# State-space stage of a hybrid encoder block on eight cores: two sets of LT broadcast tiles, and the CW/KF preparation split into two parts

## The reference, cut to what matters

```
def _s5_direction(u, lam_re, lam_im, log_dt, b_re, b_im, c_re, c_im, reverse):
    ...
    dt = jnp.exp(log_dt.astype(f32))[:, None]
    lam_bar = jnp.exp(lam * dt)
    ...
    b_bar = ((lam_bar - 1.0) / lam)[..., None] * b_mat
    ...
    bu = jnp.einsum('gph,blgh->blgp', b_bar, u.astype(jnp.complex64))
    a = jnp.broadcast_to(lam_bar, bu.shape)
    _, states = lax.associative_scan(_linear_recurrence_op, (a, bu), reverse=reverse, axis=1)
    return jnp.einsum('ghp,blgp->blgh', c_mat, states).real
```

## Time and profile before

| | us |
|---|---|
| median of 12 runs | 1573.94 |
| lowest and highest of them | 1569.84, 1695.45 |
| the profiled execution | 1569.84 |
| its span on the slowest core, from first to last instruction | 1568.7 |
| spans of the eight cores | 1561.8 to 1568.7 |

### The profile page before, as it was taken

How to read it: one execution, slowest core, us unless ns; L and a number is a source line. 1 busy time by engine, 2 the same in 40 slices (tenths; PEclk the granted TensorE clock), 3 DMA queues, 4 the chain that set the end, 5 groups by cost and what they waited for, 6 DMA issues and landing times.

```text
span 1568.7 us, 21398 instructions; the slowest of 8 cores (1561.8 to 1568.7 us)
## 1 busy us (share of the span) xinstructions
PE 1115.2 (71%) x6296; PEld 596.9 (38%) x6296; DVE 759.5 (48%) x1262; ACT 594.8 (38%) x1111; POOL 546.3 (35%) x582
## 2 busy tenths in 40 slices
PE   1988747995517731763256346488899999999995
PEld 1434313442405521552245234244344444444442
DVE  2374521113484738563756466456234443334456
ACT  2778633223314451536252625456211111111134
POOL 1000001222194638473657379300332333333231
PEclk9999979998555565565556556699899999999998
DMA  9523300000100000000000000082421430332114
GB/s 194 118 68 102 91 2 0 1 1 0 34 2 20 1 1 21 1 1 1 14 1 0 1 1 1 14 199 71 68 34 22 54 55 4 51 55 28 27 55 161
DMA packets 27377, 61.77 MB, mean 39 GB/s; under 512 B 2272, under 2 KB 11104, under 8 KB 27264
## 3 DMA queue, kind: packets, MB, share of 16 engines
q0 software_dynamic: 15408, 22.58, 10.5%
q1 hardware_dynamic: 11856, 37.82, 7.6%
HBM read 74.58 MB, written 8.39 MB: 53 GB/s over the span
## 4 chain that ended last, share of the span: by engine, by line
PE 57%; DVE 13%; ACT 13%; issue 10%; POOL 4%; DMA 2%; ACTq 0%; DVEq 0%; POOLq 0%; SPq 0%
PE p_pb L936 14%; PE p_pb L954 14%; PE p_pb L461 6%; PE p_pb L680 5%; PE p_pb L579 4%; DVE s_smb L272 4%; PE p_pb L876 4%; PE p_pb L413 2%; DMA s_w_in_bf<-w_in 2%; ACT s_CD L448 2%; PE p_pb L397 1%; PE p_pb L401 1%; DVE s_tbt L700 1%; DVE s_CD L451 1%; PE p_pb L842 1%
## 5 line engine op out<-in xcount | busy, mean ns | idle before, releaser
L958 DVE TENSOR_TENSOR s_h<-s_h,p_pb 128x512 f32<-128x512 f32 x256 | 175.7, 688 | 259.1 <-PE p_pb L954 258.2
L940 POOL TENSOR_TENSOR s_hid<-s_rl 128x512 bf16<-128x512 f32 x128 | 133.3, 1044 | 337.2 <-ACT s_rl L939 308.3
L936 PE MATMUL p_pb<-s_zffn,s_w1c 128*128 128x512 bf16 x1024 | 228.4, 382 | 3.4 <-issue 3.4
L954 PE MATMUL p_pb<-s_w2c,s_hid 128*128 128x512 bf16 x1024 | 227.8, 381 | 4.3 <-DVE s_h L958 4.3
L939 ACT ACTIVATE s_rl<-p_pb 128x512 f32<-128x512 f32 x128 | 76.2, 597 | 341.1 <-PE p_pb L936 321.7
L680 PE MATMUL p_pb<-s_u_s,s_WB 32*128 32x257 bf16 (+1 forms) x768 | 160.1, 406 | 49.4 <-ACT s_VAbig L685 46.9
L936 PEld LDWEIGHTS p_pb<-s_zffn,s_w1c 128*128 128x128 bf16 x1024 | 100.7, 98 | 126.0 <-issue 6.9
L954 PEld LDWEIGHTS p_pb<-s_w2c,s_hid 128*128 128x128 bf16 x1024 | 100.5, 98 | 126.5 <-issue 6.9
L680 PEld LDWEIGHTS p_pb<-s_u_s,s_WB 32*128 32x128 bf16 x768 | 102.2, 139 | 103.0 <-issue 57.2
L461 PE MATMUL p_pb<-s_uc,s_CD 128*128 128x512 bf16 x496 | 114.8, 394 | 32.2 <-DVE s_CD L451 32.2
L579 PE MATMUL p_pb<-s_identf,s_LTt 128*128 128x128 f32 x256 | 65.5, 437 | 86.7 <-ACT s_LTt L576 61.5
(11 more groups left out here) (153 smaller groups left out, 1793.6 us busy)
## 6 DMA issues: line engine op xcount, KB each, us to landing
s_xt<-xl SPq DMA_DIRECT2D x32, 512.0 KB, 3.8
s_h<-xl SPq DMA_DIRECT2D x16, 512.0 KB, 19.9
s_w1c<-w_ff POOLq DMA_DIRECT2D x8, 1024.0 KB, 14.1
s_w2c<-w_ff POOLq DMA_DIRECT2D x8, 1024.0 KB, 14.4
out<-s_h SPq DMA_DIRECT2D x16, 512.0 KB, 2.7
s_w_in_bf<-w_in POOLq DMA_DIRECT2D x8, 384.0 KB, 20.0
s_w_out_bf<-w_out POOLq DMA_DIRECT2D x1, 2048.0 KB, 47.3
s_bc<-b_c SPq DMA_DIRECT2D x4, 256.0 KB, 4.1
```

The lines of the kernel that those rows point to most:

```text
L936: op("pe", lambda e, k=k, f=f: e.matmul(pb[pi_][:, :], w1c[wb_][:, k, f * 128:(f + 1) * 128], zffn[:, k, blk * 512:(blk + 1) * 512], start ...
L940: op("pool", lambda e, f=f: e.tensor_tensor(hid[hb][:, f, :], rl[rb][:], rl[rb][:], op=ALU.mult), r=["rl%d" % rb], w=["hid%d_%d" % (hb, f)])
L954: op("pe", lambda e, f=f, half=half: e.matmul(pb[pi_][:, :], hid[hb][:, f, ti * 128:(ti + 1) * 128], w2c[wb_][:, f, half * 512:(half + 1) ...
L958: op("dve", lambda e, half=half: e.tensor_tensor(h[:, tt_, half * 512:(half + 1) * 512], h[:, tt_, half * 512:(half + 1) * 512], pb[pi_][: ...
```

## The change

`LTt` gets eight buffers in two sets, chosen by whether the power is even or odd, and ACT's copies for the next power are written ahead of PE's matmuls of the present one, within one half. `bc` keeps a single buffer. `prep_cwkf` gets a parameter: part "a" holds the loads, the CW products, Bb and C0 and stays behind tile 1; part "b" holds the KF matmuls, the KF copies and Dd and is written behind tile 6, which puts it behind V7 on PE and behind table 7 on ACT. The cut diff (Bb and C0 are only indented):

```diff
@@ -523,12 +523,12 @@
-            bcs = [P.sb("bc%d" % i, [128, 2, 2, 128], F32) for i in range(2)]
+            bcs = [P.sb("bc0", [128, 2, 2, 128], F32)] * 2
...
-            LTt = [P.sb("LTt%d" % i, [128, 4, 32], F32) for i in range(4)]
+            LTt = [P.sb("LTt%d" % i, [128, 4, 32], F32) for i in range(8)]
...
-                bc = bcs[jj % 2]
-                bck = "bc%d" % (jj % 2)
+                bc = bcs[0]
+                bck = "bc0"
                 if half in (None, 0):
                     P.dma("sp", bc[:], b_c_d[:, jj], w=[bck])
-                for e_ in range(8):
-                    if half is not None and e_ // 4 != half:
-                        continue
+                es = [e_ for e_ in range(8) if half is None or e_ // 4 == half]
+
+                def lt_copies(e_):
+                    for ri in range(2):
+                        for dl in range(2):
+                            li = (e_ % 2) * 4 + ri * 2 + dl
+                            qv = Qk[e_][ri]
+                            o0 = jj * 8 + dl * 4
+                            op("act", lambda e, li=li, qv=qv, o0=o0: e.copy(
+                                LTt[li][:], qv.ap[:, o0:o0 + 4].unsqueeze(2).to_broadcast([128, 4, 32])), r=[qv.key], w=["LT%d" % li])
+
+                lt_copies(es[0])
+                for e_ in es:
+                    if e_ + 1 in es:
+                        lt_copies(e_ + 1)
                     pw = e_ % 4
                     for ri in range(2):
                         for dl in range(2):
-                            lt = LTt[ri * 2 + dl]
-                            ltk = "LT%d" % (ri * 2 + dl)
-                            qv = Qk[e_][ri]
-                            o0 = jj * 8 + dl * 4
-                            op("act", lambda e, lt=lt, qv=qv, o0=o0: e.copy(
-                                lt[:], qv.ap[:, o0:o0 + 4].unsqueeze(2).to_broadcast([128, 4, 32])), r=[qv.key], w=[ltk])
+                            li = (e_ % 2) * 4 + ri * 2 + dl
+                            lt = LTt[li]
+                            ltk = "LT%d" % li
                             col = (ri * 2 + dl) * 128
                             op("pe", lambda e, lt=lt, col=col, pw=pw: e.matmul(
                                 pb[pw][:, col:col + 128], lt[:].rearrange("p a b -> p (a b)"), identf[:], start=True, stop=True),
...
-            def prep_cwkf(jj):
-                P.dma("sp", cs[:], c_s_d[:, jj], w=["cs"])
-                P.dma("sp", bs[:], b_s_d[:, jj], w=["bs"])
+            def prep_cwkf(jj, part=None):
+                if part in (None, "a"):
+                    P.dma("sp", cs[:], c_s_d[:, jj], w=["cs"])
+                    P.dma("sp", bs[:], b_s_d[:, jj], w=["bs"])
...
                 for k in range(1, 9):
+                    if part == "b":
+                        break
                     pre_, pim_ = Pk[k]
                     ce = "pool" if k % 2 == 0 else "dve"
                     Ba, Bc = (B3, B4) if k % 2 == 0 else (B1, B2)
...
+                if part == "b":
+                    pass
+                else:
+                  qre, qim = Qk[0]
+                  tt("dve", B1, bsre, bc8(qre), ALU.mult)
...
+                if part == "a":
+                    return
                 for k in range(8):
                     for dl in range(2):
                         for q in range(4):
...
@@ -764,7 +781,9 @@
                     if i < 8:
                         emit_scan(i)
                     if i == 1:
-                        prep_cwkf(jj)
+                        prep_cwkf(jj, "a")
+                    if i == 6:
+                        prep_cwkf(jj, "b")
                     if i == 3 and jj < 3:
                         prep_wb(jj + 1, 0)
                     if i == 5 and jj < 3:
```

More of the change, by code:

```diff
@@ L614, in prep_cwkf @@
                                                                        op=ALU.subtract), r=[Ba.key, Bc.key], w=[cwk])
[L615 to L626, removed]
+                if part == "b":
[3 more added lines that the diff above has]
+                  tt("dve", B1, bsre, bc8(qre), ALU.mult)
+                  tt("dve", B2, bsim, bc8(qim), ALU.mult)
+                  op("dve", lambda e: e.tensor_tensor(Bb[:, 0].rearrange("p a b c -> p (a b) c"), B1.ap, B2.ap, op=ALU.subtract),
+                     r=[B1.key, B2.key], w=["Bb"])
+                  tt("dve", B1, bsre, bc8(qim), ALU.mult)
+                  tt("dve", B2, bsim, bc8(qre), ALU.mult)
+                  op("dve", lambda e: e.tensor_tensor(Bb[:, 1].rearrange("p a b c -> p (a b) c"), B1.ap, B2.ap, op=ALU.add),
+                     r=[B1.key, B2.key], w=["Bb"])
+                  op("dve", lambda e: e.tensor_copy(C0[:, 0].rearrange("p a b c -> p (a b) c"), csre.ap), r=["cs"], w=["C0"])
+                  op("dve", lambda e: e.tensor_scalar(C0[:, 1].rearrange("p a b c -> p (a b) c"), csim.ap, -1.0, None, op0=ALU.mult),
+                     r=["cs"], w=["C0"])
+                if part == "a":
+                    return
                 for k in range(8):
```

## The result

| | us |
|---|---|
| median before (32 runs beside these) | 1573.94 |
| median after (8 runs) | 1524.35 |
| ratio, with its 95% interval | 0.9694 [0.9684, 0.9704] |
| profiled execution before, after | 1569.84, 1522.89 |
| its span before, after | 1568.7, 1521.8 |

The account below looks back on a forecast made before the run. In the state-space stage, all engines queue behind DVE's part a, and LT copies wait for PE. Gains 3.9 + 30.0 + 7.2 + 2.0 = 43.1 off 1569.84 give 1526.7; keeping the median's 4.1 distance, 1531, range 1524 to 1538.

Parts of the forecast that it names:

- First table preparation: Before the first V matmul: with two LT sets PE stays ahead and DVE sets the end; 3.9 us gained once.
- The split: KF build moved from tile 1 to tile 6: table 3's DVE step follows remod(1) at once; 7.5 us a block, 30.0 total.
- LT pairs: LT halves of blocks 0 to 2: 0.53 us gaps between matmul groups go; 1.5 plus 0.9 a block, 7.2 total.
- LT at high clock: Rival, chance 0.08: TensorE's clock rises under gapless LT matmuls, saving 6 us more, 1525, at most 12, 1519.
- The new wait: Block end: KF copies and Dd behind table 7 delay L782, L791, L804; hidden by POOL's last Sb, cost nothing.
- its signs of being wrong: In the changed profile: L804 released by L791 or ACT, POOL without idleness from tile 3, or part a above 25.2 us.
- KF at low clock: Rival, chance 0.12: block-end KF run stays at clock 0.50, taking 16.7 us; L804 5.3 us late; 24 saved, 1550.
- L804 behind a running PE: Last 128 matmuls of blocks 0 to 2 start at full clock instead of 0.50 after idleness; 0.7 each, 2.0 us.
- Part a longer: Slower rival, chance 0.04: DVE's part a operations stretch with PE and ACT beside them, up to 48 us; 1622.
- Behind the stage: Everything after the state-space stage, from block 3's L804 to the span's end: unchanged, 0 us.
- The sum of 43.1: Total gain in us: 3.9 first preparation, 30.0 KF move, 7.2 LT, 2.0 L804; taken from the profiled 1569.84.
- the two upper ends: Best cases named for the range's lower end: LT 9 us against 7.2, L804 4.5 us against 2.0.

Follow-up runs that it names:

- the early KF build: Changed kernel, but part b at tile 3: KF matmuls behind V4, copies and Dd behind the first LT half's copies; 1528.36 us, ratio 0.9717 to before.

## Why the prediction was right

**First table preparation, forecast 3.9.** The mechanism is right: from DVE's first L593 to the first V matmul it is 16.20 us (404.84 to 421.04) and was 20.14 (402.74 to 422.88), 3.94 less. But DVE's start was taken to stay where it was. The load of bc ended 5.72 us after the first LT copy here and 4.70 before, so 2.92 arrived. This core has the least of the eight: from the first LT copy to the first V matmul they took 20.36 to 21.92 us, against 24.66 to 24.84 before. In the traces of the experiments with one bc in which that load ended the wait it was 4.38 to 5.62, in the one with two 4.24. These overlap, so most of what is missing can be the load's own spread; the single buffer was not tried by itself. In the blocks it cost nothing, as forecast: ahead of the first L593 of block 1's LT half, at 622.38, DVE waits for PE's L588 and not for the load.

**The split, forecast 7.5 a block.** Measured 7.54 in block 1 by the same sum, whose terms came out at 2.17 (table 3), 1.64 (V4's copies) and 6.08 (table 4), against 2.36, 1.64 and 5.94. Nothing of DVE's or POOL's work became less; only what waited behind it did. In block 3, which has no LT half, 7.86 came of 8.2, and 0.90 of it is L804's term: 7.52 was won up to table 4's step, and 0.56 lost again behind it. Of the 43.9 us inside the stage the split has 30.2, when the other terms are taken off as measured below.

**LT pairs, forecast 2.4 a block.** Measured in block 1, from the first LT copy to the next table's DVE step: 2.2 and 0.7 for the halves, against 1.5 and 0.9. From table step to table step in blocks 0 to 2 it is 2.1, 2.1 and 1.9, then 0.5, 0.7 and 0.4: 7.7 in all, forecast 7.2. The step that failed is that PE alone sets the first half: the LT matmuls went from 0.50 to 1.00 before they were done, as the rival "LT at high clock" has it, and the 32 records took 6.76 us in block 1 (5.22 in block 0) in place of 9.79 (four times 2.05 with three gaps of 0.53). DVE then became the last: V5's remaining matmuls wait 1.93 us for its last L596, up to 630.83, since DVE's combining operations take up to 1.52 us beside POOL. So of the 3 us that PE won about 2 arrived. In block 1's second half it is DVE again that holds V7.

**The new wait, forecast at nothing, with 0.3 to 1.3 us of slack.** L801 starts 3.03 us after table 7's end (672.89 to 675.92), as forecast. L801 and L810 took 11.4 us and not 10.1 to 11.1: the clock rose at 681, 5.0 us after L801's start, where in the trace of before it rose 2.5 to 4.6 us after L782's. That used up the slack. L823 follows L810 directly in blocks 0 to 2, which the prediction had put among its signs of being wrong (L804 released by PE's own L791). It cost next to nothing: L823 starts 0.26 to 0.34 us after POOL's last Sb is complete (686.90 to 687.21 in block 1), and before the change, where PE stood waiting for it, that was 0.25 (710.58 to 710.83):

```profile
709.85 0.73 POOL L748 TENSOR_TENSOR s_Sb<-s_pt 128x258 bf16<-128x258 f32 x1
```

So at most 0.1 us a block was paid. This is the beginning of the rival "KF at low clock", and it stopped there: the 16.7 us of a run at 0.50 throughout did not come.

**L804 behind a running PE, forecast 0.7 in each of blocks 0 to 2.** It runs at 1.00 from the start, 128 matmuls in 3.75 us. From L804 to the next block's first table step it was 19.56, 20.15 and 19.64 us and is 18.74, 18.76 and 18.74: 0.8 to 1.4, 3.1 in all for a forecast of 2.0. Taken at its middle value, it was sized too low; the early KF build shows the same amount from the other side.

**Part a longer, the rival on the slower side.** 25.20 us with 7.03 us of PE and 1.88 of ACT beside it: neither slows DVE's operations by anything that shows.

**Behind the stage, forecast 0, came 4.0.** From block 3's L804 to the end it is 570.8 us here, 574.8 before, and 572.4 to 574.4 in the six experiments, which have the same code there. The change does not touch it, and the other cores of the two traces show it as spread: before, the eight cores took 569.7 to 574.8 us for this stretch, the slowest core the longest, and after the change 570.4 to 572.5; the medians are 571.6 and 570.9. For the stage, from the first LT copy to block 3's L804, the eight cores took 595.8 to 598.9 us and take 550.3 to 551.9: medians 596.3 and 551.3, 44.9 less, where the sum said 43.1.

**The sum and its range.** The sum of 43.1 stands against 43.9 inside the stage on the two slowest cores, less 1.1 by which the stage began later. The errors partly cancel: 1.0 too much for the first preparation, 0.5 and 1.1 too little for LT and L804. The distance of 4.1 us between the profiled execution and the median was kept for the changed kernel, where it is 1.5; with the 4.0 behind the stage that is the difference between 1531 and 1524, and none of it is the mechanism's. The lower end of the forecast's own range, 1524, does not follow from the two upper ends named for it: they lie 1.8 and 2.5 us beyond their terms and lead to 1526.7. That 1524.35 lies inside is luck.

## What to carry to other kernels

When one engine has a long block of work, look at what stands behind it in the queues of the other engines: moving only the consumers of its last result gave 2.3% here, with not one operation less. Then look at where the producer's operations run beside another engine's that lengthen them: moving GpSimd's half away from VectorE's, and slicing the rest, gave another 2.6%. The sliced operations took 0.42 us where GpSimd was idle and 1.13 to 1.52 beside its wide ones. A stretch of matmuls set just ahead of a late, dependent one cost at most 0.1 us a block here, since it fitted the wait, and handed over an engine at full clock.

## What the hardware showed that was not expected

- GpSimd slows VectorE by the operands, not in general. L596, one input from PSUM, takes 0.41 us beside a busy POOL (623.38); L598 of the same size, both inputs from SBUF, 1.52 (624.86). The products of part a take 0.65 to 0.95 beside POOL's 256-wide ones, 0.41 alone, and 1.13 to 1.52 beside its 514-wide ones. The Trainium skill ("SBUF — State Buffer", section "Who interferes with whom") has a VectorE instruction with two SBUF inputs contend with GpSimd's reads; these rows agree, and the factor of up to 3.7 is from them. It is not two inputs alone: C0's scaling, with one input from SBUF, took 0.63 us beside POOL in the change (L640, 606.59) and 0.29 without it where GpSimd's half had been moved (L642, 595.85).
- TensorE's clock rose under gapless float32 128x128 matmuls (L588), and stayed at 0.50 under the same ones with gaps of 0.53 us between groups of 2.05 (L579, in the run with the split alone). V5's first 16 matmuls with 32 rows, straight behind L588, still ran at 1.00 (626.85 to 628.90). After 1.93 us of waiting the next 48 of these stayed at 0.50, 9.68 busy us of the 9.80 from 630.90, as 12.90 us of them had before.
